# A list scheduler sets each engine's instruction order in a hybrid decoder layer

## What is computed

```python
h = x + 0.5 * swiglu(rms_norm(h, ffn1_norm), ffn1_w_gate, ffn1_w_up, ffn1_w_down)
u = rms_norm(h, mix_norm)
proj = u @ w_in                      # pool | q | k | v | two gates
y_pool = multiscale_pool(u_pool, pool_w, pool_scale) @ w_branch_pool
y_attn = moba_attention(q, k, v, slopes) @ w_branch_attn   # 8 heads, causal, top-3 blocks of 256
h = h + (gates[0] * y_pool + gates[1] * y_attn) @ w_out
h = h + 0.5 * swiglu(rms_norm(h, ffn2_norm), ffn2_w_gate, ffn2_w_up, ffn2_w_down)
return rms_norm(h, final_norm)
```

## Time and profile before

| | us |
|---|---|
| median of 3 runs | 6467.29 |
| lowest, highest | 6453.53, 6468.56 |
| profiled execution | 6528.1 |
| its span on the slowest core (core 1) | 6526.6 |
| its spans on the eight cores | 6421.8 to 6526.6 |
| TensorE (PE) busy | 5906.3 (90%) |
| VectorE (DVE) busy | 3105.8 (48%) |
| ScalarE (ACT) busy | 1714.3 (26%) |
| GpSimd (POOL) busy | 721.1 (11%) |

### The profile page before, as it was taken

One profiled execution on the slowest core, in us unless ns is written; L12 is line 12 of the kernel. 1 busy time (PEld: TensorE's weight loads), 2 busy tenths in 40 slices (PEclk: granted clock), 3 DMA queues, 4 the chain that ended last, 5 costly groups with the idle time before them and its releaser, 6 DMA issues.

```text
span 6526.6 us, 82897 instructions; the slowest of 8 cores (6421.8 to 6526.6 us)
## 1 busy us (share of the span) xinstructions
PE 5906.3 (90%) x26592; PEld 2609.5 (40%) x26592; DVE 3105.8 (48%) x4488; ACT 1714.3 (26%) x2569; POOL 721.1 (11%) x682
## 2 busy tenths in 40 slices
PE   5788998998999999898999999989899999989898
PEld 2333443433444443343434344434344444434333
DVE  2445454444454545444445454544345555444534
ACT  1123223133121322313312131231422223132231
POOL 2111010100111101011010110101101010110101
PEclk9899999989889999999988899999999999999999
DMA  9879553433445444343344445434344453434324
GB/s 194 203 185 211 171 162 99 155 115 119 143 136 171 143 152 153 110 152 120 133 147 137 138 139 162 143 119 147 117 141 160 149 169 130 151 127 142 116 88 142
DMA packets 296909, 944.61 MB, mean 145 GB/s; under 512 B 34140, under 2 KB 34908, under 8 KB 296284
## 3 DMA queue, kind: packets, MB, share of 16 engines
q1 hardware_dynamic: 282496, 891.42, 41.3%
q0 software_dynamic: 13104, 47.32, 4.7%
q10 hardware_dynamic: 888, 0.58, 0.1%
HBM read 905.23 MB, written 80.74 MB: 151 GB/s over the span
## 4 chain that ended last, share of the span: by engine, by line
PE 80%; DVE 6%; DMA 5%; ACT 4%; issue 3%; POOL 1%; DVEq 0%; ACTq 0%; SPq 0%; POOLq 0%
PE ps L524 18%; PE ps L486 17%; PE ps L473 17%; PE ps L568 12%; PE ps L883 3%; PE ps L774 3%; ACT PT L759 3%; PE ps L750 3%; PE ps L847 2%; PE ps L853 2%; PE ps L607 2%; DMA xp<-x 2%; DMA wscr<-wF 1%; PE ps L390 1%; DVE u L422 1%
## 5 line engine op out<-in xcount | busy, mean ns | idle before, releaser
L473 PE MATMUL ps<-u,wF 128*128 128x512 bf16 x5632 | 1395.7, 393 | 43.1 <-DMA wF<-wall 20.7
L486 PE MATMUL ps<-u,wF 128*128 128x512 bf16 x5632 | 1378.2, 389 | 37.2 <-DVE tF L491 33.1
L524 PE MATMUL ps<-hid,wF 128*128 128x512 bf16 x5632 | 1319.5, 391 | 8.4 <-DMA wF<-wall 8.4
L378 POOL TENSOR_TENSOR acc<-acc,sq 128x512 f32<-128x512 f32 x448 | 594.9, 1328 | 4875.8 <-ACT sq L377 4865.9
L568 PE MATMUL ps<-u,wM 128*128 128x512 bf16 x3584 | 878.5, 390 | 51.9 <-DVE u L422 43.2
L476 ACT ACTIVATE tF<-ps 128x512 f32<-128x512 f32 x704 | 419.8, 596 | 1835.5 <-PE ps L473 1687.2
L473 PEld LDWEIGHTS ps<-u,wF 128*128 128x128 bf16 x5632 | 564.7, 101 | 771.0 <-issue 214.4
L486 PEld LDWEIGHTS ps<-u,wF 128*128 128x128 bf16 x5632 | 559.1, 100 | 746.6 <-issue 184.4
L491 DVE SCALAR_TENSOR_TENSOR tF<-tF,ps 128x512 f32<-128x512 f32 x704 | 481.1, 683 | 785.0 <-ACT tF L476 748.6
L524 PEld LDWEIGHTS ps<-hid,wF 128*128 128x128 bf16 x5632 | 562.7, 100 | 716.4 <-issue 127.1
L493 DVE TENSOR_TENSOR hid<-tF,ps 128x512 bf16<-128x512 f32 x704 | 484.4, 688 | 604.2 <-PE ps L486 569.8
(11 more groups left out here) (74 smaller groups left out, 3473.1 us busy)
## 6 DMA issues: line engine op xcount, KB each, us to landing
wF<-wscr SPq DMA_DIRECT2D x990, 512.0 KB, 3.4
wM<-wscr SPq DMA_DIRECT2D x360, 512.0 KB, 4.5
xp<-x SPq DMA_DIRECT2D x384, 256.0 KB, 3.5
wF<-wall POOLq DMA_DIRECT2D x66, 512.0 KB, 8.9
wscr<-wF SPq DMA_DIRECT2D x66, 512.0 KB, 8.2
out<-h SPq DMA_DIRECT2D x128, 256.0 KB, 2.7
wM<-wall POOLq DMA_DIRECT2D x24, 512.0 KB, 8.9
wscr<-wM SPq DMA_DIRECT2D x24, 512.0 KB, 6.4
```

What stands on the lines that cost most here:

```text
L378: P.add("pool", lambda e: e.tensor_tensor(acc[:, a, :], acc[:, a, :], sq[:, b, :], ALU.add), reads=[("sq", b), ("acc", a)], writes=[("acc" ...
L473: ins = e.matmul(bk(b), wF[:, sl, k * 128:(k + 1) * 128], u13[:, k, :], start=(k == 0), stop=(k == 7))
L486: ins = e.matmul(bk(b), wF[:, sl, 1024 + k * 128:1024 + (k + 1) * 128], u13[:, k, :], start=(k == 0), stop=(k == 7))
L524: ins = e.matmul(bk(b), wF[:, sl, q * 128:(q + 1) * 128], hid[:, kk, :], start=(kk == 0), stop=(kk == 21))
```

## The change

After the program is emitted, and before waits are worked out, a list scheduler puts the operations in a new order (`schedule`). It builds the graph of dependences that the old order implies (every read after write, write after read, and order on a PSUM bank), gives each operation an assumed duration (`Meter` runs the operation's function on a stand-in that counts elements), and plays the program: whenever an engine comes free it takes, among its operations whose inputs are ready, the one that was emitted first; if none is ready, it waits for the next. A result is ready 120 ns after its end on another engine, a DMA 2000 ns after its bytes at 280 bytes a ns. The list is then sorted by the assumed starts, so the order is fixed when the kernel is built. No operation is added, removed or given another buffer. Besides, the key "u3" becomes "u13", so that the writes for FFN2 and the matmuls that read them depend on each other in the graph.

```diff
+class Meter:
+    def __getattr__(self, name):
+        def call(*args, **kw):
+            out = kw.get("out", args[0] if args else None)
+            n = out.free_size()
+            if name == "dma_start":
+                other = kw["in_"]
+                self.nbytes += max(out.nbytes(), other.nbytes()) if self.eng == "pool" else out.nbytes()
+                self.ns += 1000.0 if self.eng == "pool" else 60.0
+            elif name == "matmul":
+                f32 = args[1].dtype == F32
+                self.ns += max(100.0, n * 0.42) * (4 if f32 else 1)
+            elif self.eng == "act":
+                self.ns += 260.0 + 0.66 * n
+            elif self.eng == "dve":
+                if name == "tensor_reduce":
+                    n = args[1].free_size()
+                self.ns += 100.0 + n * (6.6 if name == "reciprocal" else 1.15)
+            else:
+                self.ns += 100.0 + 2.4 * n
...
-    def resolve(self):
+    def schedule(self):
+        deps_of = self.depend(True)
...
+        for _ in range(n):
+            best = None
+            for e in ENGS:
+                while wait[e] and wait[e][0][0] <= free[e]:
+                    heapq.heappush(avail[e], heapq.heappop(wait[e])[1])
+                if avail[e]:
+                    c = (free[e], e)
+                elif wait[e]:
+                    c = (wait[e][0][0], e)
+                else:
+                    continue
+                if best is None or c < best:
+                    best = c
+            t, e = best
+            i = heapq.heappop(avail[e]) if avail[e] else heapq.heappop(wait[e])[1]
+            op = self.ops[i]
+            m = Meter(e)
+            op.fn(m)
+            start[i] = t
+            free[e] = end = t + m.ns
...
+            if op.is_dma:
+                bw = max(bw, end) + m.nbytes / 280.0
+                end = bw + 2000.0
+            for j in succ[i]:
+                at = end + (0.0 if self.ops[j].eng == e and e == "pe" and not op.is_dma else 120.0)
...
+        self.ops = [self.ops[i] for i in sorted(range(n), key=lambda i: (start[i], i))]
+
+    def depend(self, every):
...
+    P.schedule()
     P.resolve()
...
-                    bg.extend(normh_apply(i, norm(3, i), 2, u13, "u3") + [lambda i=i: ready.add(("u3", i))])
+                    bg.extend(normh_apply(i, norm(3, i), 2, u13, "u13") + [lambda i=i: ready.add(("u3", i))])
```

More of the change, by code:

```diff
@@ L1 @@
 import contextlib
+import heapq
 import numpy as np
@@ L49, in __init__ @@
         self.is_out = is_out
+class Meter:
+    def __init__(self, eng):
+        self.eng = eng
+        self.ns = 0.0
+        self.nbytes = 0
+    def __getattr__(self, name):
[17 more added lines that the diff above has]
+                self.ns += 100.0 + 2.4 * n
+            return self
+        return call
 class Prog:
@@ L61, in dma @@
         self.ops.append(Op(queue, fn, reads, writes, is_dma=True, sem_key=sem_key, is_out=is_out))
-    def resolve(self):
+    def schedule(self):
+        deps_of = self.depend(True)
+        n = len(self.ops)
+        succ = [[] for _ in range(n)]
+        left = [len(d) for d in deps_of]
+        for i, d in enumerate(deps_of):
+            for j in d:
+                succ[j].append(i)
+        ready = [0.0] * n
+        free = {e: 0.0 for e in ENGS}
+        avail = {e: [] for e in ENGS}
+        wait = {e: [] for e in ENGS}
+        start = [0.0] * n
+        bw = 0.0
+        cause = [None] * n
+        self.log = []
+        for i in range(n):
+            if not left[i]:
+                heapq.heappush(avail[self.ops[i].eng], i)
+        for _ in range(n):
[18 more added lines that the diff above has]
+            free[e] = end = t + m.ns
+            self.log.append((t, end, cause[i], op))
+            if op.is_dma:
[3 more added lines that the diff above has]
+                at = end + (0.0 if self.ops[j].eng == e and e == "pe" and not op.is_dma else 120.0)
+                if at > ready[j]:
+                    ready[j], cause[j] = at, op
+                left[j] -= 1
+                if not left[j]:
+                    heapq.heappush(wait[self.ops[j].eng], (ready[j], j))
+        self.est = max(free.values())
+        self.ops = [self.ops[i] for i in sorted(range(n), key=lambda i: (start[i], i))]
+    def depend(self, every):
         last_writer = {}
@@ L93, in resolve @@
                 dop = self.ops[d]
-                if not dop.is_dma and not op.is_dma and dop.eng == op.eng and op.eng == "pe":
+                if not every and not dop.is_dma and not op.is_dma and dop.eng == op.eng and op.eng == "pe":
                     continue
@@ L97, in resolve @@
             deps_of.append(real)
+        return deps_of
+    def resolve(self):
+        deps_of = self.depend(False)
+        for real in deps_of:
             for d in real:
```

## The result

The changed kernel takes 0.918 of the time before (95% interval 0.9148 to 0.9221), which on the 6460 us of the kernel before in the same job is about 5933 us; its two executions that are compared took 5924.4 and 5941.0. The forecast was 6055 with a range from 5930, so the direction and most of the mechanism held, and the time came out 122 us lower, at the very edge of the range.

What follows compares the result with a forecast made beforehand. TensorE (PE), busy 90% of the span, was taken as the bound, with 620 us idle and lowered clock to win. 6528.1 - 150 - 71 - 174 + 0 - 87 + 10 gave about 6055 us, range 5930 to 6340.

Steps and rivals of the forecast that it cites:

- norms' waits: PE's waits at L390 for GpSimd's add into acc, now mostly covered by sixteen or more matmuls: -150 us (-120 to -162).
- half clock: PE at the 1.2 GHz level after norm gaps; 45 fewer gaps save 1.58 us each: -71 us (-45 to -90).
- attention's waits: PE's 229.4 us for exponential, PV bank emptying and mask DMAs, mostly covered by other matmuls: -174 us (-115 to -215).
- K projection: PE's 43.2 us wait for u2 stays, with 72 matmuls ahead in both orders: 0 us (-43 to +20).
- 0.81 stretches: Stretches at granted clock 0.81, if PE restarts trigger them, fall from four to one: -87 us (-112 to 0).
- start: At the kernel's start, x loads on SP wait behind weight stores: +10 us (-20 to +40).
- The first: Rival: misjudged durations bring back half the norm, attention and half-clock gains, 198 us: 6253 or 6340 us; chance 0.18.
- The second: Rival: PE without pauses is held at 0.81 behind the first 250 us, +1191: 7250 us; chance 0.09.
- The third: Rival: no change, PE's idle moves from L390 and L774 to F banks and u2: 6450 to 6487 us; chance 0.03.

Runs made afterwards that it cites:

- the run with the adds kept off: Changed kernel, but GpSimd's adds of squares planned near the eight u2 writes wait for the last of them: ratio 0.900, 5827 and 5829 us.
- the key's run: Kernel before with only the key u3 changed to u13, emission order, no scheduler: ratio 0.9966, 6448 to 6465 us.
- the barrier run: Changed kernel, but every norm matmul is a barrier in PE's order, as in the emission order: repeat measured at ratio 0.9419, 6082 to 6101 us.
- writes that yield: Changed kernel, but VectorE takes u2 writes only when nothing else of its work is ready: ratio 0.9023, 5835 and 5837 us.

## Why the prediction came out 122 us high

The sum was made from core 1 of before (6526.6); here it stands against core 6 of after (5939.4). The clock terms are read in windows of 2 us behind the first 250 us (half clock where PEclk is below 0.75, 0.81 where it is from 0.75 to 0.99), and count only time in which PE was busy, so that no time stands in a wait and in a clock term both.

| term | predicted | measured |
|---|---|---|
| norms' waits | -150 | -159 (162.5 to 3.3) |
| half clock | -71 | -82 (122 to 40) |
| attention's waits | -174 | about -225 (229.4 to 4) |
| K projection | 0 | +70 (43.2 to 113.5) |
| 0.81 stretches | -87 | -90 (122 to 32) |
| start | +10 | 0 (103.2 to 103.6, idle of PE up to 250 us) |
| F banks (not in the sum) | | -31 (33 to 2) |
| busy time per stop (not in the sum) | | about -55 (an estimate, see below) |

These make -572 of the -587; the rest has no name. That the time stayed inside the range is partly luck: attention and the K projection both left their bounds (-215 and +20), in opposite directions, and without the K projection's growth (the run with the adds kept off, 5827) it would have fallen below 5930.

**Norms** were right, by their own steps: sixteen or more matmuls of cover are enough, and what little is left (3.1 us at the kernel's last norm) lies where the prediction put it. **Half clock** was right for what it priced, the norms' stops: with the norm matmuls alone free (core 3) it falls to 54 us, from 131 in the key's run (core 4). But with the norms' stops kept (core 0 of the barrier run) it falls to 77 as well, by stops of attention and the F banks that I had priced at nothing, and the K projection's longer stops give some 20 back (40 here, 20 with the adds kept off). That the net came out near -71 is in part luck.

**Attention was sized too low.** I counted 15 us that the new PE order falls short, then left 55 for ScalarE running in order. That reserve was not needed. With PE's matmuls in the old order the other engines' new orders alone took the exponential's wait from 117 to 63 us, and with ScalarE in its old order PE's freedom kept it at 13.8: either covers much of the wait, and PE's order nearly all.

**The K projection is the step that failed**, and in the wrong direction. The count of 72 matmuls was right and so was the VectorE excerpt; the step that missed was pricing the eight writes by rows in which no add runs beside them, and taking the order of one engine at a time. The new order of squares and adds puts the next norm's adds beside those writes. The upper bound of +20 had no mechanism in it. Three ways of removing the meeting or covering it (adds later, ScalarE's old order, writes that yield) took the wait to 40.3, 40.0 and 38.7 us, near the 43.2 that the prediction left standing.

**Not in the sum: the F banks**, 33 us of waits of the ups, were below the rows that I had weighed, and the prediction only used them as a place where idle time could go to. **And the busy time.** PE stood still in 386 windows of 2 us between 250 and 5500 us before and in 86 after (less than 1.7 us busy). Between two cores without 0.81 stretches and with all 26592 matmuls in the trace (core 4 of the key's run, 5811.0 busy, and core 1 of the changed kernel, 5657.5), busy time falls by 153 us, of which the lower clock accounts for 91 (windows below 0.75) to 106 (every step of the granted clock). The 47 to 62 left over some 317 stops are 0.15 to 0.20 us each, near the 0.17 that the earlier trace rows show for a QK pair that is not followed at once (0.60 where two in a stream take 0.43). This is an estimate; no run isolates it. The number was in my own rows, and I priced stops by their idle time and the slow clock alone.

**The 0.81 stretches**: the size was right, the reason was not, so the size was luck. On cores 6 and 7 of the changed kernel a stretch begins at 5748, 214 us after PE's last stop of more than 0.3 us, which I had said did not happen. And cores 2 and 4 of the kernel before had none from 250 to 6400 us in the same execution, with about 400 stopped windows each. No core had one in the profile with the norm matmuls alone free (303 to 319 stopped windows a core between 250 and 5500 us), nor in the one with the adds kept off (47 to 53). So a stop does not set one off by itself. What does set it off stays open. The term was a property of the profiled execution (6528 against a median of 6467) and mostly should have been taken out of the base.

**The start** cost little: the first gate began at 60.2 us on core 6 (62.9 on core 1, 54.5 before), under the 65 that I had set, and the first K projection came at 257 and 261 us, where it had come at 254 and 259 (cores 1 and 2 of the kernel before).

**Rivals.** The first is a real mechanism with about the price that I gave: 0.6 of the durations costs 260 us, my half of the waits was 198. In one place it came true: it named VectorE sharing time with GpSimd, and that is the K projection's +70. Elsewhere the assumed times are near the chip's (tanh 598 ns assumed, 597 measured; L583 689 and 686; the adds 1329 and 1365), and the runs whose times are 0.6 and 1.6 of these are slower, so this nearness is the likely reason that the waits stayed away. The second, unbroken PE held at 0.81, is contradicted, in the executions compared here, by windows of 140 us that were fully busy at 1.00 (below). The third is out.

## What to carry to other kernels

A fixed order from a list scheduler is worth its name when its durations are near the chip's; where two engines share something, price the pair, not each, and look at what the *other* engines now do at the same moment. Price a stop of the bound engine by its idle time, the slow clock behind it and the time that the restart adds to its busy time. A reordering is one thing over all queues: here SP's order alone could undo nearly all of it, and ScalarE's old order was better than the new one, because it kept GpSimd's adds off VectorE's writes.

## What the runs showed of the hardware

A VectorE write with two SBUF inputs beside a GpSimd add took 1748 ns instead of 745. From 2292 us on core 6 each add takes 1.47 us, one every 1.67 (back to back in the run with the adds kept off, 1.26 or 1.27 us, one every 1.42 to 1.47), and the writes too begin 1.67 or 1.68 us apart, 0.26 or 0.27 behind an add: the two took turns.

Unbroken matmuls on all eight cores at full clock are possible. The window of core 1 of the changed kernel (PE, PEld, DVE, ACT, POOL busy, PEclk, DMA share, GB/s); on the other cores PE is busy for 139.0 to 139.9 at 1.00:

```profile
5600.00:5740.00 140.00, 139.87 (x681) 64.87 (x679) 54.21 (x74) 71.19 (x91) 0.00 (x0) 1.00 0.30 98
```

The limiter rule of the Trainium skill (TensorE: Matmul & The Clock Gate, Part 1) would have both dies at 13/16 here; these rows, of one execution, do not agree. Some 10 us later two cores of one die fell, and a third did not (core 6, then core 5, the columns as above):

```profile
5748.00:5752.00 4.00, 4.00 (x18) 1.68 (x17) 1.38 (x2) 1.78 (x3) 2.97 (x3) 0.85 0.08 13
5760.00:5800.00 40.00, 39.74 (x149) 16.53 (x150) 30.44 (x46) 5.50 (x9) 5.78 (x4) 0.81 0.38 126
...
5748.00:5752.00 4.00, 4.00 (x19) 1.77 (x17) 0.69 (x1) 1.74 (x3) 2.72 (x3) 1.00 0.35 131
```

Cores 6 and 7 fell together, as cores 0 and 1, and 6 and 7, did before.
